# A two-layer hybrid decoder kernel: page copies spread over attention, early-turned key steps taken together, value weights split early, a fourth value slot

## The chip, the cores and the metric

The kernel runs on one NeuronCore of a Trainium2 chip. Time is device microseconds (us) of one execution; three executions of the kernel before took 1945.38 to 1946.76 us, median 1946.29. A further execution was taken by the hardware profiler; it took 1943.64 us, and its trace covers a span of 1942.0 us.

The engines are called by the profile's names: PE (TensorE, matrix products) and PEld (its weight loads), DVE (VectorE), ACT (ScalarE), POOL (GpSimd) and SP (SyncE). SP and POOL issue nearly all DMA transfers, each on a queue of its own: the profile calls SP's q1 and POOL's q0.

## The reference

Two layers of a decoder work on 512 prompt rows and on 32 sample rows (8 sequences of 4 tokens). Each has a combined input projection, a retention branch, a block-sparse attention branch (MoBA) with rotary positions, two gates, an output projection and a SwiGLU feed-forward part. Only the attention of the sample rows reads the paged cache:

```python
def moba_sample(q, k_new, v_new, k_pages, v_pages, page_table):
    ...
    def one(q_b, kn_b, vn_b, pt_b):
        ...
            k_full = k_pages[pt_b[:n_full * ppb]].reshape(n_full, M_BLOCK, M_HEADS, M_DH)
            means = jnp.mean(k_full.astype(jnp.float32), axis=1).swapaxes(0, 1)
            idx, valid = moba_select(qh, means, n_full_q, k_sel)
            phys = pt_b[idx[..., None] * ppb + jnp.arange(ppb)]
            kg = k_pages[phys, :, hidx].reshape(M_HEADS, L, k_sel, M_BLOCK, M_DH)
            vg = v_pages[phys, :, hidx].reshape(M_HEADS, L, k_sel, M_BLOCK, M_DH)
        return moba_core(qh, kg, vg, valid, k_own, v_own, own_mask)
```

Each sequence has 8 pages of 128 tokens (8 heads of 64, fp32), so a page is 256 KB. All scores of all pages are computed; the choice of blocks (3 of 4 for each head and query) is made on the scores, and blocks that are not chosen get a large negative bias before the softmax. The new keys and values of prompt and sample are outputs of their own (`k_prompt`, `v_prompt`, `k_sample`, `v_sample`).

## The kernel before, in words

**Products.** fp32 products are made as three products of rounded parts: high weight with high input, low weight with high input, high weight with low input. A *unit* of weights (1024 rows by 256 columns) is loaded into one of two slots of `RAW` by SP (`full`, L536 on), its high part `WH` is written by ACT and its low part `WL` by DVE (the two calls named `split`, L1472 and L2023). A unit then serves five *tiles* of outputs, four of 128 prompt rows (24 matmuls each) and one of the 32 sample rows (16 short ones, `sample_part`, L817). The units of the first half of a layer are, in this order: `mqk` (4 units), `mv` (2), `rqa` (1), `rv` (4), `rqb` (3), then `br_att` and others.

**Page copies.** A step `r` of keys (16 in a layer, r = 0 to 15) takes one page of each of 4 sequences. POOL copies each page of keys from the cache to a DRAM tensor `keys_laid` in another layout (`lay_keys`, L673 to L679), 64 copies in a layer, and counts their landings in two semaphores, one for the 12 copies of steps 0 to 2 (`FIRST_STEPS`, 3) and one for the other 52. In layer 0 they stand at the start (L683 to L686): the first 12 wait for nothing, the others for the tiles of `mqk` and `mv`, two copies to a tile. Layer 1's copies are made during layer 0's feed-forward part. After layer 0's 64 copies stand, in POOL's queue, the writes of the outputs `k_prompt`, `v_prompt`, `k_sample` and `v_sample` (L690 to L697).

**Key steps.** SP loads a laid step (1 MB) into one of four buffers (`keys(r)`, L567 to L576; buffers `PG` twice, `XT`, `PGK`), DVE turns it in place (`turned(r)`, L2095 to L2098), and PE multiplies it with the sample queries (`key_scores(q)`, L1069 to L1083). Steps 0 to 2 are loaded and turned before attention begins. `keys(3)` waits for all 52 later copies and for the last scores of the prompt's attention; `keys(r)` from 4 on waits for PE's `key_scores(r - 4)`.

**Order around the change.** All of it is written out by hand for each engine. After `mv`, PE transposes the rotated queries and keys (L952, L955), then runs the prompt's attention in 16 steps (`scores`, L1007; `turn_probs`, L1021; `attend`, L1037) with the tiles of `rqa` between them. ACT makes the exponentials (`exp`, L1529) and waits before the first one for the landing of `k_prompt` (L1536), since the probabilities overwrite its source. After the last attention step PE runs 16 key steps with tiles of `rv` between them (`value_rows`, which gives the tiles of a step), then 16 value steps (`attend_sample`, L1112) with tiles of `rqb` between them. The bank of an `rqa` tile is freed by ACT (`to_rotate`, L1494) into one of two buffers, which DVE then rotates (`rotated`, four instructions, L2050 to L2055). `attended(3)` (L1540 on ACT, L2136 on DVE) splits the last attention output into parts.

**Value steps.** `values` (L509 to L523) loads the value pages of a step into one of three slots, two sequences by SP and two by POOL; from step 3 on each load waits for PE's value step three before it. `own_head` (L2197) and `to_columns` (L1126) finish a group of 4 sequences.

## Time and profile before

| | |
|---|---|
| Three executions | 1945.38, 1946.29, 1946.76 us |
| Profiled execution, its own time | 1943.64 us |
| Span of its trace | 1942.0 us |
| PE busy | 1904.5 us, 98% |
| DVE, ACT, POOL busy | 1331.9, 815.6, 203.9 us |
| DMA, whole span | 300.60 MB, mean 155 GB/s |
| Chain that ended last | PE 66%, DVE 5%, issue, DMA and ACT 1% each |

Busy time of PE is time in which some matmul is under way; the rest of the span, some 37 us, is time in which PE had nothing. A matmul record is longer than the distance between two matmuls, since they overlap, so distances between starts are used for what work costs. In a row of a timeline the first number is the start, the second the length of the merged piece, and what stands in brackets is how long the engine was idle before it and what ended that idle time.

### The profile page before, as it was taken

How to read it: one execution, taken by the hardware profiler on the slowest of the kernel's cores; microseconds unless marked ns; L12 is line 12 of the kernel's file. 1: busy time of each engine (PE TensorE's matmuls, PEld its weight loads, DVE VectorE, ACT ScalarE, POOL GpSimd, SP SyncE). 2: the span in 40 equal slices, each digit the busy share in tenths (PEclk: the TensorE clock that was granted, in tenths of full speed). 3: DMA queues.
4: the chain of work that ended last, by engine and by line, in shares of the span. 5: the costliest groups of instructions: out<-in, count | busy, mean ns of one | idle time of the engine just before them, and what ended most of it. 6: DMA issues, size and time to landing. Idle time of an engine off the chain costs nothing.

```text
span 1942.0 us, 39546 instructions
## 1 busy us (share of the span) xinstructions
PE 1904.5 (98%) x16267; PEld 1784.2 (92%) x16267; DVE 1331.9 (69%) x1902; ACT 815.6 (42%) x1287; POOL 203.9 (10%) x293
## 2 busy tenths in 40 slices
PE   8889999999999999999999999999999999999999
PEld 8867978999999999999999688799899999999998
DVE  6466744347765988988665775543686668889876
ACT  4344333323434454554433632233244345455453
POOL 2520020012000002112100002100110000000000
PEclk9999999999999999999999999999999999999999
DMA  7944883246244346656453278622642442433332
GB/s 244 353 156 159 298 288 104 68 150 220 77 155 133 87 126 182 182 161 185 137 190 134 63 249 285 219 72 83 210 139 93 150 133 77 144 94 103 100 102 85
DMA packets 274852, 300.60 MB, mean 155 GB/s; under 512 B 14538, under 2 KB 225650, under 8 KB 274162
## 3 DMA queue, kind: packets, MB, share of 16 engines
q1 hardware_dynamic: 249202, 207.48, 34.0%
q0 software_dynamic: 25344, 90.46, 14.1%
q8 instruction: 129, 2.11, 0.5%
q14 instruction: 49, 0.40, 0.1%
q10 hardware_dynamic: 128, 0.15, 0.0%
HBM read 273.00 MB, written 58.59 MB: 171 GB/s over the span
## 4 chain that ended last, share of the span: by engine, by line
PE 66%; DVE 5%; issue 1%; DMA 1%; ACT 1%; POOL 0%; SPq 0%; POOLq 0%; DVEq 0%; ACTq 0%
PE PS L913 26%; PE PS L1378 22%; PE PS L1289 3%; PE PS L893 2%; PE PS L894 1%; PE PS L895 1%; PE PS L872 1%; PE PS L873 1%; PE PS L874 1%; PE PS L1082 1%; PE PS L817 1%; PE PS L1112 1%; PE PS L1037 1%; PE PS L1432 0%; PE PS L1007 0%
## 5 line engine op out<-in xcount | busy, mean ns | idle before, releaser
L2023 DVE TENSOR_TENSOR WL<-RAW,WH 128x2048 fp32r<-128x2048 f32 (+2 forms) x76 | 161.0, 2119 | 68.0 <-ACT WH L1472 68.0
L913 PE MATMUL PS<-XH,WH 128*128 128x272 f32 x960 | 203.2, 293 | 0.6
L913 PE MATMUL PS<-XL,WH 128*128 128x272 f32 x960 | 198.4, 288 | 0.0
L913 PE MATMUL PS<-XH,WL 128*128 128x272 f32 x960 | 197.8, 287 | 0.0
L1472 ACT ACTIVATE WH<-RAW 128x2048 fp32r<-128x2048 f32 (+2 forms) x84 | 149.8, 1783 | 34.7 <-PE PS L913 18.5
L1378 PE MATMUL PS<-KQ,CH 128*128 128x272 f32 x1088 | 158.3, 288 | 1.4 <-DVE KQ L2609 1.4
L913 PEld LDWEIGHTS PS<-XH,WH 128*128 128x128 f32 x960 | 150.4, 188 | 7.8 <-issue 5.2
L893 PE MATMUL PS<-WH,XH 128*128 128x256 f32 x512 | 152.3, 297 | 4.5 <-ACT EA L1494 4.5
L913 PEld LDWEIGHTS PS<-XL,WH 128*128 128x128 f32 x960 | 150.9, 188 | 0.0
L913 PEld LDWEIGHTS PS<-XH,WL 128*128 128x128 f32 x960 | 150.3, 189 | 0.0
L1378 PEld LDWEIGHTS PS<-KQ,CH 128*128 128x128 f32 x1088 | 145.0, 188 | 2.2 <-issue 2.2
L894 PE MATMUL PS<-WL,XH 128*128 128x256 f32 x512 | 145.9, 285 | 0.0
L895 PE MATMUL PS<-WH,XL 128*128 128x256 f32 x512 | 145.0, 283 | 0.0
L893 PEld LDWEIGHTS PS<-WH,XH 128*128 128x128 f32 x512 | 97.5, 190 | 31.7 <-issue 27.6
L678 POOL DMA_DIRECT2D keys_laid<-in_cache_k x128 | 95.3, 744 | 212.7 <-issue 198.1
L872 PE MATMUL PS<-WH,XH 128*128 128x256 f32 x336 | 96.7, 288 | 5.4 <-ACT EA L1505 5.4
L895 PEld LDWEIGHTS PS<-WH,XL 128*128 128x128 f32 x512 | 98.2, 192 | 0.0
L894 PEld LDWEIGHTS PS<-WL,XH 128*128 128x128 f32 x512 | 97.6, 191 | 0.0
L873 PE MATMUL PS<-WL,XH 128*128 128x256 f32 x336 | 96.1, 286 | 0.0
L874 PE MATMUL PS<-WH,XL 128*128 128x256 f32 x336 | 95.3, 284 | 0.0
L1859 ACT ACTIVATE EB<-PS 128x272 f32<-128x272 f32 x96 | 38.1, 397 | 129.7 <-PE PS L1378 127.6
L2621 DVE TENSOR_TENSOR CH<-RAW,CH 128x1536 fp32r<-128x1536 f32 x44 | 77.2, 1755 | 12.5 <-ACT CH L1841 12.5
(462 smaller groups left out, 5116.0 us busy)
## 6 DMA issues: line engine op xcount, KB each, us to landing
RAW<-in_w_in SPq DMA_DIRECT2D x94, 512.0 KB, 5.8
keys_laid<-in_cache_k POOLq DMA_DIRECT2D x128, 256.0 KB, 4.5
RAW<-in_w_gu SPq DMA_DIRECT2D x128, 256.0 KB, 4.3
PG<-keys_laid SPq DMA_DIRECT2D x16, 1024.0 KB, 6.5
RAW<-in_w_down SPq DMA_DIRECT2D x64, 256.0 KB, 4.3
RAW<-in_w_gu SPq DMA_DIRECT2D x24, 512.0 KB, 5.1
PG<-in_cache_v POOLq DMA_DIRECT2D x44, 256.0 KB, 4.8
PG<-in_cache_v SPq DMA_DIRECT2D x44, 256.0 KB, 4.5
```

The lines of the kernel that those rows point to most:

```text
L678: pool.dma_start(KEYS.ap()[lay, r, b].rearrange("(g k) (c d) -> (k c) g d", g=4, c=4), src.rearrange("p (g d) -> p g d", g=4)).then_inc(ke ...
L872: pe.matmul(out, a, wh[:, k], start=k == 0, stop=False)
L873: pe.matmul(out, a, wl[:, k], start=False, stop=False)
L874: last = pe.matmul(out, b, wh[:, k], start=False, stop=k == KT - 1)
L893: pe.matmul(out, a, wh[:, k], start=k == 0, stop=False)
L894: pe.matmul(out, a, wl[:, k], start=False, stop=False)
L895: last = pe.matmul(out, b, wh[:, k], start=False, stop=k == KT - 1)
L913: last = pe.matmul(PS[:, 2 * pair + h, 0:HALF], w[:, i, c0:c0 + P], block[:, h * HALF:(h + 1) * HALF], start=first and i == 0 and a == 0, ...
L1378: last = pe.matmul(PS[:, bank, 0:HALF], a[:, k, :], moving(n - 1, k, low), start=start and k == m == 0, stop=k == HK - 1 and m == 2, skip_ ...
L1472: act.activation(WH[:, slot, 0:n], RAW[:, slot, 0:n], ACT.Copy).then_inc(hi_ready, 1)
L2023: dve.tensor_tensor(WL[:, slot, 0:n], RAW[:, slot, 0:n], WH[:, slot, 0:n].bitcast(F32), ALU.subtract).then_inc(lo_ready, 1)
L2621: dve.tensor_tensor(a_part(s, 1), raw_chunks(s % 2)[:, 1:4], a_part(s, 0).bitcast(F32), ALU.subtract).then_inc(la_ready, 1)
```

## The change

Five things change, in both layers unless it is said otherwise.

1. Layer 0's page copies. The first 34 of the 64 are issued during `mqk` and `mv`; the first 12 of them now wait for tiles too, two to a tile, and from the 13th on it is one to a tile rather than two. The other 30 (`late`) stand behind the writes of the four outputs and wait for the prompt's attention scores, two to a step.
2. PE runs the key steps 0, 1 and 2 one after the other, then the last `rqa` tile, then `rv` tiles, 19 of them spread evenly over key steps 3 to 15.
3. The first `rv` unit is split before attention: ACT before its first exponential, DVE between taking the norm factors and the first reciprocals. The later splits move from key steps 1, 5, 9, 13 to 4, 7, 10, 14.
4. DVE waits for the last attention product, rotates three tiles and then does `attended(3)`; ACT does `to_rotate(2)` before its `attended(3)`. In the value steps `own_head(0)` stands ahead of the rotation of step 8.
5. Value step 3 goes to a fourth slot (`PGK`), with all four sequences loaded by SP; the steps from 4 on use the three slots in turn, and steps 4 to 6 wait for value steps 0 to 2.

```diff
-        return V_STEP // 4 * 16 + (32 * len(range(slot, V_STEP, 3)) if slot < 3 else 0)
+    def value_place(v):
+        return v if v < 4 else (v - 4) % 3
...
     def value_rows(q):
-        return [q - 1 + u for u in range((q + 3) // 4 - (q % 4 == 1), (q + 3) // 4 + 1)] if q else []
+        n = V_STEP - FIRST_STEPS
+        return range((q - FIRST_STEPS) * (4 * TT - 1) // n, (q + 1 - FIRST_STEPS) * (4 * TT - 1) // n) if q >= FIRST_STEPS else ()
...
-            if v < 3:
+            if v < 4:
                 hold(eng, sc_done, scores_done(lay, V_STEP - 4 + v))
-            for b in seqs:
-                if v >= 3:
-                    hold(eng, pvs_page, lay * 64 + 4 * (v - 3) + b + 1)
+            for b in seqs if v != 3 else range(GRP) if eng is nc.sync else ():
+                if v >= 4:
+                    hold(eng, pvs_page, lay * 64 + 4 * (v - (4 if v < 7 else 3)) + b + 1)
...
-                for at_r, name, j, col in ((4, "rv", 1, C_RV), (7, "rv", 2, C_RV), (10, "rv", 3, C_RV),
+                for at_r, name, j, col in ((4, "rv", 1, C_RV), (7, "rv", 2, C_RV), (11, "rv", 3, C_RV),
...
-        for i in range(GRP * V_STEP):
-            if i >= GRP * FIRST_STEPS:
-                hold(pool, tile_done, T0["mqk"] + 2 + (i - GRP * FIRST_STEPS) // 2)
+        early, late = GRP * FIRST_STEPS, 2 * 15
+        for i in range(GRP * V_STEP - late):
+            hold(pool, tile_done, T0["mqk"] + (i // 2 if i < early else i - early // 2))
             lay_keys(0, i)
...
+            for i in range(late if lay == 0 else 0):
+                hold(pool, s_done, i // 2 + 1)
+                lay_keys(0, GRP * V_STEP - late + i)
             values(pool, lay, (2, 3), page_in_b)
...
-                if q == 1:
+                if q == FIRST_STEPS:
                     token_part("rqa", 4, kk)
...
+            split(U0["rv"], 1, 8 * UC, (tile_done, lay * NT + T0["rqa"]))
             act.wait_ge(kp_out, lay * 16 + 16)
...
-            attended(3)
...
             to_rotate(2)
+            attended(3)
             to_rotate(3)
-            split_at(U0["rv"])
...
-                if q in (1, 5, 9, 13):
-                    split_at(U0["rv"] + (q + 3) // 4)
+                if q in (4, 7, 10, 14):
+                    split_at(U0["rv"] + (q - 1) // 3)
...
             take_rt(2 * lay + 1, (6, 7))
+            split(U0["rv"], 1, 8 * UC)
...
-            attended(3)
...
+            dve.wait_ge(pv_done, lay * 4 + 4)
             rotated(0)
             rotated(1)
             rotated(2)
-            split_at(U0["rv"])
+            attended(3)
             rotated(3)
             turned(3)
...
             for i in range(V_STEP):
+                if i == 8:
+                    own_head(0)
                 for f in late_rows(i):
                     rotated(f)
```

On DVE, at the end of the prompt's attention, the program before has these rows (`MOL` is the low part that `attended` writes, the `EA` and `RQ` rows are one `rotated`, `WL` is a split, `PGK` the turn of key step 3; two more rotations stand before the split and one behind it):

```order
L2136 TENSOR_TENSOR MOL<-PS,MOH 128x512 x2
L2050 SCALAR_TENSOR_TENSOR EA<-EA,CL 128x128
L2051 TENSOR_TENSOR EA<-EA,CL 128x128
L2052 TENSOR_TENSOR EA<-EA,CL 128x256
L2055 TENSOR_TENSOR RQ<-EA 128x256
...
L2023 TENSOR_TENSOR WL<-RAW,WH 128x2048
...
L2097 STREAM_TRANSPOSE PGK<-PGK 128x2048
```

The changed program has at the same place (`MOL` at L2149, a rotation at L2063 to L2068; between the first rotation and the second `MOL` row stand two more):

```order
L2149 TENSOR_TENSOR MOL<-PS,MOH 128x512
L2063 SCALAR_TENSOR_TENSOR EA<-EA,CL 128x128
L2064 TENSOR_TENSOR EA<-EA,CL 128x128
L2065 TENSOR_TENSOR EA<-EA,CL 128x256
L2068 TENSOR_TENSOR RQ<-EA 128x256
...
L2149 TENSOR_TENSOR MOL<-PS,MOH 128x512
L2063 SCALAR_TENSOR_TENSOR EA<-EA,CL 128x128
...
L2110 STREAM_TRANSPOSE PGK<-PGK 128x2048
```

The split is gone from this place, the second `MOL` stands behind three rotations, and the turn of key step 3 has four rotations and a `MOL` ahead of it.

On PE, at the end of the prompt's attention, the program before goes on as follows (`PT,MV` is the last attention product, `QB` rows are key steps, the `WH` row begins the last `rqa` tile and `RAW,XT` is the sample tile of `rv`):

```order
L1037 MATMUL PS<-PT,MV 64x128 [waits pt_evac]
L1037 MATMUL PS<-PT,MV 64x128 x7
L1082 MATMUL PS<-PG,QB 32x128 [waits s_exp,kt_turned]
L1082 MATMUL PS<-PG,QB 32x128 x15
L893 MATMUL PS<-WH,XH 128x256 [waits tile_free,lo_ready]
...
L817 MATMUL PS<-RAW,XT 32x256 [waits xn_ready,tile_free,lo_ready]
```

The changed program:

```order
L1049 MATMUL PS<-PT,MV 64x128 x7
L1094 MATMUL PS<-PG,QB 32x128 [waits s_exp,kt_turned]
L1094 MATMUL PS<-PG,QB 32x128 x15
L1094 MATMUL PS<-PG,QB 32x128 [waits kt_turned]
...
L1094 MATMUL PS<-XT,QB 32x128 [waits kt_turned]
...
L905 MATMUL PS<-WH,XH 128x256 [waits tile_free,lo_ready]
...
L829 MATMUL PS<-RAW,XT 32x256 [waits xn_ready,tile_free,lo_ready]
L829 MATMUL PS<-RAW,XT 32x256 x7
L1094 MATMUL PS<-PGK,QB 32x128 [waits kt_turned]
```

Key steps 1 and 2 stand directly behind step 0, and key step 3 (`PGK`) behind one `rqa` tile and the sample tile of `rv`.

On POOL the changed program of layer 0 has, where before a last copy stood ahead of `out<-QK` and value loads behind `out<-MVS`:

```order
L687 DMA keys_laid<-in_cache_k 128x4x128
L699 DMA out<-QK 128x4x512 [waits rot_free]
L702 DMA out<-MV 128x4x512 [waits tile_free]
L705 DMA out<-XT 32x512 [waits own_act]
L706 DMA out<-MVS 32x512
L518 TENSOR_LOAD PTAB [waits s_done]
```

The last row begins the first of the 30 late copies.

## Rows read from the trace of the kernel before

**Rows 1.** The page: busy us of each engine, share of the span, instructions.

```profile
PE 1904.5 (98%) x16267; PEld 1784.2 (92%) x16267; DVE 1331.9 (69%) x1902; ACT 815.6 (42%) x1287; POOL 203.9 (10%) x293
```

**Rows 2.** Waits of PE: in total, times, longest, us.

```profile
PE PS L1007 <- ACT PR L1529: 6.8, 6, 5.1
PE PS L872 <- ACT EA L1505: 5.4, 1, 5.4
PE PS L893 <- ACT EA L1494: 4.5, 2, 2.3
...
PE PS L1112 <- DMA PG<-in_cache_v: 2.1, 2, 1.1
...
PE PS L817 <- DVE WL L2023: 1.9, 2, 1.0
...
PE PS L1126 <- DVE OS L2197: 1.4, 2, 0.7
...
PE PS L1112 <- DMA XT<-in_cache_v: 0.3, 1, 0.3
```

**Rows 3.** Timeline of PE: start, length, idle before.

```profile
110.78 1.04 PE L980 MATMUL PS<-XT,STK 128*32 128x512 f32 x2
...
164.93 1.08 PE L1082 MATMUL PS<-PG,QB 128*32 128x128 f32 x32
...
168.28 0.36 PE L893 MATMUL PS<-WH,XH 128*128 128x256 f32 x1 [2.27 <-ACT EA L1494]
...
173.71 1.07 PE L817 MATMUL PS<-RAW,XT 128*32 128x256 f32 x16 [1.04 <-DVE WL L2023]
...
1063.02 1.05 PE L980 MATMUL PS<-XT,STK 128*32 128x512 f32 x2
...
1111.25 1.08 PE L1082 MATMUL PS<-PG,QB 128*32 128x128 f32 x32
```

**Rows 4.** Timeline of ACT: the two long waits of layer 0.

```profile
59.03 1.91 ACT L1472 ACTIVATE WH<-RAW 128x2048 fp32r<-128x2048 f32 x1 [12.36 <-DMA RAW<-in_w_in]
...
121.50 0.37 ACT L1529 ACTIVATE PR<-PS,SM 128x128 f32<-128x128 f32 x1 [9.05 <-DMA out<-QK]
```

**Rows 5.** Timeline of POOL: the last copy, then the first output.

```profile
113.61 0.74 POOL L678 DMA_DIRECT2D keys_laid<-in_cache_k  x1 [0.40 <-issue]
114.35 0.81 POOL L690 DMA_DIRECT2D out<-QK  x1
```

**Rows 6.** Stretches: busy us of PE, PEld, DVE, ACT, POOL; PEclk, DMA share, GB/s.

```profile
61.50:67.00 5.50, 5.50 (x28) 5.26 (x32) 5.19 (x14) 1.13 (x3) 3.50 (x5) 0.50 1.03 394
...
169.70:173.00 3.30, 2.97 (x15) 2.67 (x13) 2.26 (x3) 1.92 (x2) 0.00 (x0) 0.50 0.26 102
...
300.00:306.00 6.00, 4.76 (x43) 2.35 (x35) 2.79 (x7) 0.82 (x3) 0.00 (x0) 1.00 0.61 207
```

**Rows 7.** Timeline of DVE at the end of layer 0's attention.

```profile
165.68 0.69 DVE L2136 TENSOR_TENSOR MOL<-PS,MOH 128x512 fp32r<-128x512 f32 x1 [7.25 <-ACT MOH L1540]
...
167.67 0.29 DVE L2050 SCALAR_TENSOR_TENSOR EA<-EA,CL 128x128 f32<-128x128 f32 x1
...
174.77 2.30 DVE L2097 STREAM_TRANSPOSE PGK<-PGK 128x2048 f32<-128x2048 f32 x1
```

**Rows 8.** The page copies issued from 29 to 57 us: shortest, median, longest ns.

```profile
L678 POOL DMA_DIRECT2D keys_laid<-in_cache_k x22: 742/742/923, 30.2 to 56.8; - x22
```

**Rows 9.** The page's DMA issues: KB each, median us from issue to landing.

```profile
keys_laid<-in_cache_k POOLq DMA_DIRECT2D x128, 256.0 KB, 4.5
...
PGK<-keys_laid SPq DMA_DIRECT2D x8, 1024.0 KB, 7.5
```

**Rows 10.** DMA queues from 30 to 60 us: packets, MB, share.

```profile
q1 hardware_dynamic: 4103, 5.52, 53.2%
q0 software_dynamic: 1610, 5.29, 46.2%
```

**Rows 11.** DVE's groups from 113 to 165 us.

```profile
L2149 DVE TENSOR_SCALAR PR<-PR,SM 128x128 f32<-128x128 f32 (+3 forms) x32 | 10.9, 384 | 0.6
```

More of the change, by code:

```diff
@@ L449, in key_buf, with values_before, slot_values @@
         return PAGE_BUFS[q % 4]
-    def slot_total(slot):
-        return V_STEP // 4 * 16 + (32 * len(range(slot, V_STEP, 3)) if slot < 3 else 0)
+    def value_place(v):
+        return v if v < 4 else (v - 4) % 3
+    def values_before(v):
+        return [value_place(w) for w in range(v)].count(value_place(v))
+    def slot_values(slot):
+        return [value_place(v) for v in range(V_STEP)].count(slot)
     def key_landings(lay, q):
-        return lay * slot_total(q % 4) + (q // 4 + 1) * 16
+        return lay * (V_STEP // 4 * 16 + (32 * slot_values(q % 4) if q % 4 < 3 else 64)) + (q // 4 + 1) * 16
     def value_slot(lay, v):
-        slot, landed_b = v % 3, 32 * len(range(v % 3, V_STEP, 3))
-        return (slot, PAGE_BUFS[slot], lay * slot_total(slot) + V_STEP // 4 * 16 + (v // 3 + 1) * 32,
-                lay * landed_b + (v // 3 + 1) * 32)
+        slot = value_place(v)
+        landed_b = 32 * (lay * slot_values(slot) + values_before(v) + 1)
+        return slot, PAGE_BUFS[slot], (lay + 1) * V_STEP // 4 * 16 + landed_b * (2 if v == 3 else 1), landed_b
     def scores_done(lay, q):
@@ L1109, in attend_sample @@
                 pe.wait_ge(page_in[slot], landings)
-                pe.wait_ge(page_in_b[slot], landings_b)
+                if slot < 3:
+                    pe.wait_ge(page_in_b[slot], landings_b)
                 for b in range(GRP):
@@ L2233, in _ @@
             for q in range(V_STEP):
-                if q in (1, 5, 9, 13):
-                    split_at(U0["rv"] + (q + 3) // 4)
+                if q in (4, 7, 10, 14):
+                    split_at(U0["rv"] + (q - 1) // 3)
                 if q == N_PAGES:
@@ L2253, in _ @@
                     sample_probs_turned(1)
-                if i == 8:
-                    own_head(0)
                 if i == 10:
```

## The prediction, written before the changed kernel ran

> **What bounds the kernel now.** The page comes first: PE is busy for 98% of the span [rows 1], and the change leaves the work of every matmul as it is. So it can give back only two things: time in which PE stands idle, about 37 us in all (the span less PE's busy time), and time in which its clock is at the lower of its two levels. The list of PE's waits says where the idle time is; the reader is to see seven rows that lie in the stages the change touches [rows 2]. The timelines of PE and ACT then give each one its place and its cause.
>
> - A. Layer 0, before its 15th tile: PE waits 5.44 us for ACT, and ACT has waited 12.36 us for a unit of weights [rows 2, 4]. POOL issued 22 page copies in the 26.6 us before it [rows 8], and from 30 to 60 us both queues moved about the same, 5.52 and 5.29 MB, at 99% of the engines' time [rows 10].
> - B. Layer 0, first exponentials: ACT stands 9.05 us until `k_prompt` has landed [rows 4]. POOL could issue that write only at 114.35, behind its 64th copy [rows 5]. PE loses 5.1 us to it [rows 2].
> - C. After attention, both layers: 2.27 us for ACT's freeing of an `rqa` bank, then some 1 us for the split of the first `rv` unit [rows 2, 3]. ACT had to wait for DVE's first rotation, which stands behind `attended(3)`, and DVE for ACT's high part of that output [rows 7].
> - D. `to_columns(0)` waits 0.7 us in each layer for `own_head`; value pages cost 2.1 and 0.3 us [rows 2].
>
> The stretches tell what a long stall costs on top: after A (61.5 to 67) and after C (169.7 to 173) the granted clock is 0.50, that is 1.2 of 2.4 GHz; after the 1.1 us stall for a value page at 300 to 306 it stays at 1.00 [rows 6].
>
> **The copies (B).** In the changed order 34 copies stand ahead of `k_prompt` instead of 64, and the 34th waits for the 27th of 30 tiles, three tiles of 2.9 us before the transposes. The write is issued before 100 us, where the old one needed 121.5 - 114.4 = 7.1 us to land [rows 4, 5], and is there before ACT asks for it at about 113. What is late next? Layer 1 shows it, since its copies are made elsewhere and it has no such wait: from the last sample product ahead of attention to the first key step takes 1111.25 - 1063.02 = 48.2 us there and 164.93 - 110.78 = 54.2 us in layer 0 [rows 3]. I take layer 1's length for layer 0: **5.9 us** gained, with the clock's share in it. Bounds: 5.1 (the wait alone) and 6.9 (what ACT loses, were all of it PE's).
>
> What the thirty late copies cost: they have nobody behind them on POOL but value loads that come 75 us later. Their customer is `keys(3)` on SP. POOL starts them at about 113.6; in the stretch shown POOL needs (56.8 - 30.2) / 21 = 1.27 us a copy, 38 us for thirty, about as long as attention's 16 steps last, so POOL sets the pace and the thirtieth is issued by 113.6 + 30 x 1.27 = 151.7 and landed 4.5 us later, at 156.2 [rows 8, 9]. The first key step would now be at 159.0 (110.8 + 48.2). `keys(3)` lands 7.5 us after its issue, at 163.7 [rows 9]; DVE wants it at 159.0 + 5.9 = 164.9 (next part). It is in time with 1.2 us to spare, so I cost this at nothing; every us beyond is a us of PE. The first twelve copies' new waits are met before POOL comes to them.
>
> **The copies (A).** Do fewer copies bring the late weights sooner? The 13th to 20th copy wait for the 6th to 13th tile, done by the time POOL, at 1.27 us a copy, gets there; the 21st waits for the 14th, after which PE stops, 5.4 us before ACT's split and the release behind it, at about 56 [rows 2, 4]. Before, the 22nd went out at 56.8 [rows 8]. So until 56 the load is the same, what is then queued lasts for several us more (5.29 MB in 30 us is a copy in 1.5 us), and the weights landed at 59.0 [rows 4]. I take **0** here; bounds 0 and 8.2 us: 5.4, and 2.8 for the 5.5 us at half clock behind it [rows 6]. The trace has the two queues in nearly equal parts while both have work [rows 10]. The Trainium skill says why (DMA: Bandwidth & Descriptors, Queues, rings and completion order): each DMA engine goes round the queue rows that have work, a packet at a time. By that rule too a shorter copy queue helps only from the moment it runs empty, which is after these weights have landed; the trace agrees as far as it goes.
>
> **Key steps 0 to 2 together, the early split, DVE's order (C).** From the first key step to the first `rv` tile took 173.71 - 164.93 = 8.78 us [rows 3]. The work in it is one key step of 1.0 and one `rqa` tile. That tile ran 168.28 to 172.67, of which 1.4 us at full clock and 3.0 at half: 2.9 us of full clock. So 8.78 - 3.9 = 4.9 us are lost, clock included; layer 1 has both waits too [rows 2].
> Now, counted from the first key step: PE has three key steps (3.0), the tile (2.9) and the sample tile of `rv` (1.0), and comes to key step 3 at 6.9. ACT needs one rotation of DVE to free the bank, at about 2.0, before the tile's turn at 3.0; the `rv` unit is split since attention. What is late next is the turn of key step 3. DVE starts its first rotation when the last attention product ends, at 0.1. A rotation takes 1.38 from start to start (166.29 to 167.67, where 166.29 is the `MOL` start plus the 0.61 before its successor) and 1.2 when something independent follows; so three take 4.0, `attended(3)` 0.6, the fourth 1.2, and the turn starts at 5.9 and ends at 8.2 [rows 7]. PE waits 8.2 - 6.9 = 1.3 us where it lost 4.9: **3.6 us a layer, 7.2 in all**. Bounds for the new wait: 0, and 2.3, the longest wait of the old place [rows 2].
> Does a stall of 1.3 us lower the clock? 2.27 did, 1.1 did not [rows 2, 6]; 1.3 is nearer to the second. I take no; each lowering would cost 1.7 us (3.3 us at half clock) [rows 6].
> The split moved ahead of attention costs ACT 1.9 us before its first exponential and DVE 2.3 us before its first reciprocals. It lies beside the `rqa` tile of 2.9 us that PE runs there, and DVE's next task, the maximum of step 2, waits for PE's scores after that tile. I take 0, bounds 0 and 1 us a layer. The later splits have two key steps of lead, 8 us against 4.2.
>
> **Value steps (D).** `own_head(0)` no longer stands behind a rotation of 1.2 us: **1.4 us** for both layers. The wait of 0.3 us is for value step 5 of layer 1, which is now asked for one step earlier: **0.3 us**. The 2.1 us are for the last step, whose load still waits for value step 12: nothing. Bounds for these together 0 and 3.8.
>
> **Sum.** 5.9 + 7.2 + 1.4 + 0.3 = 14.8 us. Against the profiled execution's 1943.64 that is 1928.8; the median of the runs is 2.65 us higher, 1946.29, so I forecast **1931.5 us**.
>
> **Rivals.**
> 1. *The new stalls before key step 3 lower the clock.* For it: 2.27 us did. Against: 1.1 us did not. Both layers: 3.4 us back, 1934.9.
> 2. *The weights of A come sooner.* For it: POOL's queue has half the traffic, so anything that thins it before 41 us would do. Against: the 21st copy is the first that is held. 8.2 us more, 1923.3.
> 3. *Layer 0's attention does not become layer 1's.* `k_prompt` is still late, or exponentials and copies disturb each other; B gives nothing: 1937.4.
> 4. *The late copies hold up key step 3: slower.* Their end governs `keys(3)`. With 1.2 us to spare, each us later costs PE one. The gain is eaten when they end 14.8 + 1.2 = 16 us late, at 1.27 + 16/30 = 1.8 us a copy; 3.9 us more, 1950.2, at 1.93. For it: no trace shows copies beside attention. Against: 742 ns is both the shortest and the median record of a copy, under full DMA load [rows 8].
> 5. *DVE's scalings hold POOL up, in part.* DVE scales the probabilities 32 times in attention, 10.9 us [rows 11]. If POOL can't work beside them, the copies end 10.9 us later and PE waits 10.9 - 1.2 = 9.7 us more: 1941.2. For it: POOL's waits of this kind would show nowhere before. Against: POOL's 22 copies ran beside a busy DVE without a slow one [rows 8]. The Trainium skill has such a rule (SBUF — State Buffer, SBUF: two separate sides): while DVE runs an operation in a two-port mode, GpSimd can't write the descriptors of its transfers. No row here shows a copy beside such a scaling.
>
> **How the numbers follow.** Forecast 0.66, its own range 1929 to 1934 (B's and D's bounds, and the wait from 0 to 2.3). Rival 1: 0.10. Rival 2: 0.06. Rival 3: 0.06. Rival 4: 0.05. Rival 5: 0.07. Ends of the range: 1926.5, which keeps a part of rival 2, and 1938.5, which takes in rivals 1 and 3. About 0.2% (3.9 us) is what a measurement can tell from no change. Faster: all but rival 4 and a worse form of rival 5, 0.93; same 0.03; slower 0.04.
>
> **What would show it.** Right: `k_prompt` lands before 108 us and ACT has no DMA wait before the first exponential; the distance of B's two landmarks is near 48 us in both layers; the last late copy lands before 157; the key step from `PGK` has an idle time of about 1.3 us on PE, ended by DVE's turn, and no half clock behind it; the wait before the 15th tile is still 5.4 us; `to_columns(0)` waits no more. Wrong: a DMA wait ahead of that turn on DVE in layer 0 (rival 4), PE's clock at 0.50 at about 168 or 1110 us (rival 1), a shorter wait of ACT for its fourth unit (rival 2), or new waits among the `rv` tiles, where I have seen none.

## The result, and the profile after

The changed kernel takes **1925.3 us** (median of 4 runs: 1926.76, 1924.51, 1924.94, 1925.65), the kernel before beside it 1945.84 (1943.08 to 1946.76); ratio 0.9898 (of the means, as all ratios here), 95% interval 0.9881 to 0.9915. The forecast was 1931.5 and its range ended at 1926.5: the direction held and so did the mechanisms that were named, but the gain was larger by 6.2 us.

The profiled execution took 1926.76 us, its span is 1925.1. The page, as in [rows 1]:

```profile
PE 1897.3 (99%) x16267; PEld 1781.5 (93%) x16267; DVE 1332.1 (69%) x1902; ACT 814.2 (42%) x1287; POOL 201.4 (10%) x289
```

PE's idle time fell from 37.5 to 27.8 us, and PE's busy time fell too, by 7.2 us, with the same 16267 matmuls: that second part is clock and something else, which the experiments name. PE's waits, against [rows 2]:

```profile
PE PS L884 <- ACT EA L1518: 5.4, 1, 5.4
...
PE PS L1094 <- DVE PGK L2110: 2.8, 2, 1.4
PE PS L1019 <- ACT PR L1542: 2.4, 6, 0.5
PE PS L1125 <- DMA XT<-in_cache_v: 2.2, 2, 1.4
```

The wait A before the 15th tile stands as it was. The 5.1 us before the first exponentials, the waits of 2.27 and 1.0 us after attention and the two for `own_head` are gone. What is new is the wait of 1.4 us before key step 3 (line 1094, once a layer), and the last value step's page, now in `XT`. The timeline of PE gives the landmarks of [rows 3]:

```profile
109.33 1.05 PE L992 MATMUL PS<-XT,STK 128*32 128x512 f32 x2
...
157.66 1.96 PE L1094 MATMUL PS<-PG,QB 128*32 128x128 f32 x64
...
165.93 1.08 PE L1094 MATMUL PS<-PGK,QB 128*32 128x128 f32 x32 [1.41 <-DVE PGK L2110]
...
1050.25 1.04 PE L992 MATMUL PS<-XT,STK 128*32 128x512 f32 x2
...
1098.46 1.95 PE L1094 MATMUL PS<-PG,QB 128*32 128x128 f32 x64
...
1230.39 1.07 PE L1125 MATMUL PS<-XT,PTS 128*32 128x512 f32 x8 [1.44 <-DMA XT<-in_cache_v]
```

With the same landmarks of before, the two profiled executions compare so (us; "key and value part" runs from the first key step to the first transpose of the retention queries, at 303.69 and 1250.23 before, 290.96 and 1232.37 after):

| stretch | before | after | gained |
|---|---|---|---|
| start to the last sample product, layer 0 | 110.78 | 109.33 | 1.45 |
| attention, layer 0 | 54.15 | 48.33 | 5.82 |
| key and value part, layer 0 | 138.76 | 133.30 | 5.46 |
| from there to layer 1's attention | 759.33 | 759.29 | 0.04 |
| attention, layer 1 | 48.23 | 48.21 | 0.02 |
| key and value part, layer 1 | 138.98 | 133.91 | 5.07 |
| rest | 691.77 | 692.73 | -0.96 |
| span | 1942.00 | 1925.10 | 16.90 |

The loss of 0.96 at the end has a place. Behind the 1.44 us wait for the last value page the granted clock of PE was at the lower of its levels for a while, and not at all behind the 1.41 us wait before key step 3. Columns: busy us of PE, PEld, DVE, ACT, POOL; granted clock (0.5 is 1.2 of 2.4 GHz), DMA share, GB/s, as in [rows 6].

```profile
1232.40:1235.80 3.40, 3.40 (x22) 3.40 (x18) 1.54 (x3) 0.69 (x2) 0.00 (x0) 0.51 0.00 1
165.00:169.00 4.00, 3.07 (x49) 2.87 (x50) 3.97 (x6) 0.07 (x1) 0.00 (x0) 1.00 0.99 364
```

POOL's timeline and then DVE's answer to [rows 5, 7]. `k_prompt` is issued at 96.81 (it landed at 103.1), before ACT's first exponential at 112.71, which waits for no DMA. The thirty late copies go out from 112.95 to 148.07, one in 1.21 us. DVE's rotations start when attention ends, and its turn of the page for key step 3 at 163.57:

```profile
96.81 0.81 POOL L699 DMA_DIRECT2D out<-QK  x1
...
112.95 0.77 POOL L687 DMA_DIRECT2D keys_laid<-in_cache_k  x1 [0.62 <-issue]
...
148.07 0.78 POOL L687 DMA_DIRECT2D keys_laid<-in_cache_k  x1 [0.59 <-issue]
```

DVE, the first rotation and the turn:

```profile
157.78 0.29 DVE L2063 SCALAR_TENSOR_TENSOR EA<-EA,CL 128x128 f32<-128x128 f32 x1 [6.55 <-PE PS L1049]
...
163.57 2.30 DVE L2110 STREAM_TRANSPOSE PGK<-PGK 128x2048 f32<-128x2048 f32 x1
```

### The profile page after: what moved, and what is told of

It is laid out like the page before. It is cut to its first block and busy times, and to the rows that moved or that the text cites. A ratio compares the mean times of both kernels' runs of the same rounds, so it can differ in the third digit from the quotient of the medians.

```text
span 1925.1 us, 39547 instructions
## 1 busy us (share of the span) xinstructions
PE 1897.3 (99%) x16267; PEld 1781.5 (93%) x16267; DVE 1332.1 (69%) x1902; ACT 814.2 (42%) x1287; POOL 201.4 (10%) x289
```

## Experiments

Waits and clocks below are those of each kernel's profiled execution; times are medians. Over all five sets the kernel before gave medians of 1945.84, 1942.75, 1943.05, 1943.08 and 1941.68 (single runs from 1938.11 to 1947.49), so single executions scatter by some 9 us, and medians of 4 to 15 of them by 4. In the text, *half clock* is a stretch with a granted clock of 0.5.

**The changed kernel again** (no edit).

> The changed kernel once more, for a second profile and more times beside the kernel before. Theory M (the parts add up: copies 5.8 us, key steps 4.5 us a layer, own_head 1.4, value slots about 0): the mean gain is 17 to 20 us. The profiled changed run lost 1.1 us to a half-clock piece behind a 1.44 us value wait of layer 1. Theory L (that piece is a matter of the single execution): the same wait of 0.7 to 1.5 us is there again, the half clock behind it may be missing, and the run is then about 1.5 us shorter. Rival: the wait of 1.44 always lowers the clock, the piece is there again and the time is 1926.5 again.

1924.51 us against 1942.75, ratio 0.9901 (0.9886 to 0.9916): 18.2 us, inside theory M's 17 to 20. In its profile the last value step of layer 1 waited 1.91 us, and the lower clock behind it lasted twice as long:

```profile
1230.80 1.07 PE L1125 MATMUL PS<-XT,PTS 128*32 128x512 f32 x8 [1.91 <-DMA XT<-in_cache_v]
```

The stretch behind it, with the columns of [rows 6]:

```profile
1232.60:1239.40 6.80, 6.80 (x45) 5.53 (x42) 2.36 (x6) 1.37 (x4) 0.00 (x0) 0.50 0.00 1
```

Of the retention transposes behind it, the stretch up to 1240.86 took 7.90 us, where the same took 5.39 in a profile without a fall of the clock. The first profile of the same kernel has 6.54 there. So theory L is half right: from one execution to the other the wait grew by 0.5 us and the cost of the clock from 1.15 to 2.5. But the half clock came again, as the rival had it; that such a wait can stand without it shows only further down, with the write of x moved.

**The copies alone** (the kernel before, with the edits to `lay_keys`' two loops only).

> The kernel before with only the copies of layer 0 spread out. Theory M: 5.8 us faster than before (ratio 0.9970), all of it between the last sample product ahead of attention (110.8 us in before) and the first key step: that distance falls from 54.2 to 48.3 us; ACT's wait for the landing of k_prompt is gone. Rival (the copies' spreading also frees the start or the weights before tile 15): more than 7 us. Rival (it only helps together with the rest, as the first key steps wait for something): under 3 us. The waits of 2.27 and 1.0 us after attention stay.

1935.27 us, ratio 0.9956 (0.9943 to 0.9970), 5.8 to 11 us. The interval alone would leave room for the rival above 7 us, the landmarks don't: attention of layer 0 took 48.33 us (110.07 to 158.40) where it took 54.15, 5.8 us, as in the changed kernel, and the start ahead of it gained 0.7. The waits after attention stayed, the second of them longer than before:

```profile
161.75 0.36 PE L896 MATMUL PS<-WH,XH 128*128 128x256 f32 x1 [2.27 <-ACT EA L1497]
...
167.18 1.32 PE L820 MATMUL PS<-RAW,XT 128*32 128x256 f32 x16 [2.34 <-DVE WL L2026]
```

The copies are independent of the rest, and their price is the one read from layer 1. The longer second wait is not their doing: it is 2.33 us in the profile of the value steps alone, too, where the copies are as before. And behind the first of the two, of 2.27 us, the clock did not fall here, as it did in [rows 6]; it fell only behind the second:

```profile
161.75:167.40 5.65, 3.31 (x28) 3.05 (x32) 4.47 (x9) 2.75 (x3) 0.00 (x0) 1.00 0.44 168
```

**The key steps alone**, on the kernel before: PE's order, and DVE's (ACT's has the same two moves), with the new `value_rows` and the split times that go with it.

```diff
-                if q == 1:
+                if q == FIRST_STEPS:
                     token_part("rqa", 4, kk)
...
+            split(U0["rv"], 1, 8 * UC)
             for s in range(16):
...
-            attended(3)
...
             rotated(2)
-            split_at(U0["rv"])
+            attended(3)
```

> The kernel before with only the three key steps together, the early split of the first value unit, DVE's and ACT's attended(3) behind three rotations, and the new spread of the rv tiles over the key steps. Theory M: 9.0 us faster (ratio 0.9954): 3.5 a layer from the waits (4.9 lost before, 1.4 new) and 1.0 a layer from three fewer changes between dense tiles and the narrow matmuls of the key steps, at 0.3 us each. Rival (my predicted sum): 7.2 us, the rest of the gain came from somewhere else, as from the value part. The new 1.4 us wait before key step 3 is there in both layers, without half clock.

1932.66 us, ratio 0.9950 (0.9937 to 0.9964), 9.7 us. The new wait of 1.40 us is there in both layers without a fall of the clock. The key and value part of layer 0 took 133.43 us instead of 138.76: 5.3 us, of which 0.9 from the last value page (its wait was 0.19 us, before 1.08) and **4.4 from the edit**, not the 3.6 that I had worked out. Where PE isn't waiting, these stretches show it as busy; in the kernel before:

```profile
164.93:303.69 138.76, 133.69 (x1557) 108.71 (x1555) 83.51 (x136) 39.40 (x70) 17.57 (x32) 0.99 0.81 270
```

in the changed one:

```profile
157.66:290.96 133.30, 131.15 (x1557) 107.75 (x1555) 81.32 (x135) 37.47 (x69) 16.18 (x30) 1.00 0.84 285
```

and in this one it is 131.14. The same 1557 records of matmuls take 133.7 or 131.1 us. About 1.6 of the 2.5 is the half clock of [rows 6] (3.3 us at half speed). The other 0.9 went with the order: in the timelines I count 29 blocks of dense tiles between the narrow matmuls of the key and value steps before, and 25 after. One such change of work, in the changed kernel's timeline (start, length):

```profile
283.11 1.06 PE L1125 MATMUL PS<-PG,PTS 128*32 128x512 f32 x8
284.11 0.38 PE L905 MATMUL PS<-WH,XH 128*128 128x256 f32 x1
284.33 0.28 PE L906 MATMUL PS<-WL,XH 128*128 128x256 f32 x1
284.45 0.28 PE L907 MATMUL PS<-WH,XL 128*128 128x256 f32 x1
...
286.95 0.27 PE L907 MATMUL PS<-WH,XL 128*128 128x256 f32 x1
287.16 1.06 PE L1125 MATMUL PS<-PG,PTS 128*32 128x512 f32 x8
```

Dense matmuls start every 0.12 us. The first of a block takes 0.22, and the first narrow one behind a block starts 0.21 after the last dense one: 0.1 and 0.1 us lost, 0.2 a block, shown nowhere as a wait. It is so at all 25 blocks of this stretch. A new tile inside a block costs nothing of the kind, 0.11 us from the last matmul of one to the first of the next, so the loss belongs to the change of work and not to the start of a tile:

```profile
194.13 0.27 PE L907 MATMUL PS<-WH,XL 128*128 128x256 f32 x1
194.24 0.28 PE L905 MATMUL PS<-WH,XH 128*128 128x256 f32 x1
```

What in PE takes the 0.2 us no run shows.

**The value steps alone** (fourth slot and `own_head(0)` ahead, on the kernel before).

> The kernel before with only the fourth value slot and own_head(0) ahead of the late rotation. Theory M: 1.4 us from to_columns, which waits no more; the value slots give between 0 and 0.5: 1.4 to 1.9 us faster (ratio 0.9991), under what can be told from no change. Rival (the fourth slot gives earlier landings that shorten the waits of 1.0 us at the last value steps): 3 us. The last value step still waits 0.7 to 1.5 us for its page in both.

1941.35 us against 1942.75, ratio 0.9995 (0.9984 to 1.0006): no difference that can be told. `to_columns` waits no more, 1.4 us; but in this profile the last value pages came later:

```profile
302.96 1.06 PE L1121 MATMUL PS<-XT,PTS 128*32 128x512 f32 x8 [2.00 <-DMA XT<-in_cache_v]
```

That wait and the half clock behind it (304.0 to 310.8 us) ate the gain.

**The write of x behind the fourth unit of weights.** Wait A was still whole. ACT's row for it, in the changed kernel:

```profile
58.17 1.91 ACT L1485 ACTIVATE WH<-RAW 128x2048 fp32r<-128x2048 f32 x1 [12.32 <-DMA RAW<-in_w_in]
```

On SP's queue a write stands ahead of the weights that ACT waits for; in the list of DMA issues from 29 to 60 us (KB, us to landing):

```profile
x_kept<-XT SPq DMA_DIRECT2D x1, 2048.0 KB, 21.2
```

The edit puts it behind them:

```diff
                 full(U0["mqk"] + 2 + j, j, w_in, KT, C_MQ + (2 + j) * UC)
-                if j == 0:
+                if j == 1:
                     sp.dma_start(XTD.ap()[:, :, 0:SEQ], XT[:, :, 0:SEQ]).then_inc(xt_kept, 16)
```

> The changed kernel with the write of x to its DRAM copy (2.1 MB) behind the fourth unit of weights instead of ahead of it on SP's queue. Theory Q (the weights before the 15th tile are late because of what stands ahead of them in their own queue, which moves about 0.18 MB a us beside POOL's copies): they land about 10 us sooner, PE's wait of 5.4 us is gone and the half clock behind it (6.8 us at half speed, some 2 to 3 us lost) too: 6 to 8 us faster than the changed kernel, ratio to before about 0.986. Rival (the write only moves the lateness to the next units, the mv weights at 82 us): a new wait of 3 to 5 us on PE before the 20th tile or later.

1918.63 us, ratio 0.9874 (0.9849 to 0.9899): 6 to 7 us under the changed kernel's two medians, 5 by the ratios. The split now waits for nothing, and key step 3 comes at 157.90 instead of 165.93, 8.03 us sooner, of which 5.40 are the wait and some 2.3 the 4.5 us of work at half clock behind it:

```profile
45.31 1.90 ACT L1485 ACTIVATE WH<-RAW 128x2048 fp32r<-128x2048 f32 x1
```

The half clock from 58.2 to 65.0 is gone with the wait, and nothing came late instead. Its last value step in layer 1 waited 1.43 us, as long as in the changed kernel, this time at full clock:

```profile
1222.26 1.06 PE L1125 MATMUL PS<-XT,PTS 128*32 128x512 f32 x8 [1.43 <-DMA XT<-in_cache_v]
```

The stretch behind it has a granted clock of 1.00:

```profile
1224.20:1227.60 3.40, 3.24 (x40) 3.02 (x40) 1.77 (x4) 1.37 (x4) 0.00 (x0) 1.00 0.01 4
```

**The early copies thinned.**

```diff
-            hold(pool, tile_done, T0["mqk"] + (i // 2 if i < early else i - early // 2))
+            hold(pool, tile_done, T0["mqk"] + (i if i < early else 15 + (i - early) // 2))
```

> The changed kernel with the early copies thinner: the first twelve one for each tile, the next 22 only from the 15th tile on, two a tile, so that ten fewer copies (2.6 MB) are issued before PE's wait at 55 us. Theory Q2 (the copies and the weights share the engines, half each): the weights land some 5 us or more sooner, PE's wait falls from 5.4 us to under 1 and its half clock goes: 5 to 8 us faster than the changed kernel. Rival (what is ahead in the weights' own queue decides, the copies don't matter): still 4 us or more of wait. Rival (the copies now end too late for k_prompt): ACT waits at 113 us again.

1920.89 us, ratio 0.9879 (0.9853 to 0.9906). The wait A fell from 5.4 to 0.5 us, its half clock went, and `k_prompt` was in time. So either end works: what stands ahead in the weights' own queue, or what runs beside it in the other. A wait of 1.09 us for the last value page did lower the clock here:

```profile
1224.03 1.07 PE L1125 MATMUL PS<-XT,PTS 128*32 128x512 f32 x8 [1.09 <-DMA XT<-in_cache_v]
```

The stretch behind that one, at 0.51:

```profile
1226.20:1229.60 3.40, 3.40 (x19) 3.40 (x19) 1.54 (x3) 0.69 (x2) 0.00 (x0) 0.51 0.00 0
```

**One rv tile more ahead of key step 3.**

```diff
-        return range((q - FIRST_STEPS) * (4 * TT - 1) // n, (q + 1 - FIRST_STEPS) * (4 * TT - 1) // n) if q >= FIRST_STEPS else ()
+        cuts = [0] + [max(2, j * (4 * TT - 1) // n) for j in range(1, n + 1)]
+        return range(cuts[q - FIRST_STEPS], cuts[q + 1 - FIRST_STEPS]) if q >= FIRST_STEPS else ()
```

> The changed kernel with one dense rv tile more ahead of key step 3, taken from the step behind it. Theory: the wait of 1.4 us before key step 3 is DVE's chain of rotations, and PE has 2.9 us of other work for it: the wait is gone in both layers, 2.8 us faster than the changed kernel; one change between dense and narrow matmuls fewer gives 0.3 a layer more: 3.4 in all. Rival (the key step waits for its page by then or the next steps are late instead): under 1.5 us.

1923.72 us, ratio 0.9899 (0.9874 to 0.9924): in time within the scatter of the changed kernel. The wait of 1.40 us went and a wait of 0.75 for DVE's turn of a later page came, in both layers: 0.65 us a layer, not 1.7. DVE's chain of turns is what is late, and moving one tile moves the place. The number of blocks stayed at 25, against what I had expected.

```profile
169.51 1.08 PE L1095 MATMUL PS<-PG,QB 128*32 128x128 f32 x32 [0.75 <-DVE PG L2111]
```

**Three value slots again, all else as changed.**

> The changed kernel with three value slots again, all else as changed (own_head(0) ahead of the late rotation too). Profiles so far: with three slots the last value step waited 0.2 to 1.1 us (1.08, 0.97, 0.66, 0.19, 0.82) without a half-clock piece behind it; with four 0.65 to 2.0 us (0.75, 1.44, 0.65, 1.91, 2.00, 1.07) and three times a half-clock piece. Theory F (the fourth slot lengthens the last wait): waits under 1.1 us in both layers, no half clock there, 1 to 3 us faster than the changed kernel (1922 to 1924). Theory L (the waits scatter, whatever the slots): waits and time as of the changed kernel, within 1 us.

1925.81 us, ratio 0.9905 (0.9888 to 0.9921): as the changed kernel. Theory F's gain of 1 to 3 us did not come, and the fourth slot is worth nothing that can be told in time. The waits for the last page were small here (0 and 0.50 us, and 0.80 at value step 5 of layer 1), as F had it; the combination below that has three slots too waited 1.37 us and lost clock. Theory L's "whatever the slots" isn't borne out by the profiles either: the last page cost 0.5 to 2.05 us in both layers together in the five with three slots, 1.1 in the mean, and 1.4 to 3.1 us, 2.2 in the mean, in the seven with four slots and no hold. That part of F stays open.

```profile
1230.69 1.06 PE L1116 MATMUL PS<-PG,PTS 128*32 128x512 f32 x8 [0.50 <-DMA PG<-in_cache_v]
```

**SP's later weights held until value step 14 is done.**

```diff
             values(sp, lay, (0, 1), page_in, next_unit)
+            hold(sp, pvs_page, lay * 64 + 4 * (V_STEP - 2) + 4)
             full(U0["br_att"] + 1, 1, w_br_att, 4, 0)
```

> The changed kernel with SP's weights behind the value loads (br_att unit 1 and all after it) held until value step 14 is done, so that they don't move beside the last page. Theory W (these weights take engines from POOL's two loads of the last page, which land last, at 1228.3 and 1230.25 us): the last wait falls by 0.7 us or more in both layers. Rival (POOL's loads are late by their own issue and the distance from step 12): no change. Cost of the hold, if the weights come late for the gate tiles: a new wait 20 us later.

1922.82 us, ratio 0.9892 (0.9875 to 0.9908), a time within the scatter of the changed kernel. Both last waits are gone and no new one came. In layer 1 the step (line 1126, `XT`) follows its neighbour directly:

```profile
1226.62 1.06 PE L1126 MATMUL PS<-PG,PTS 128*32 128x512 f32 x8
1227.50 1.04 PE L1126 MATMUL PS<-XT,PTS 128*32 128x512 f32 x8
```

POOL's two loads of this page in layer 1 took 6.0 us to land in the changed kernel, where they are issued at 1222.73 and 1223.91, and 3.6 us here, issued at 1221.46 and 1222.64; the lists of DMA issues have, first for the changed kernel (1220 to 1232 us), then for this one (1218 to 1230 us):

```profile
XT<-in_cache_v POOLq DMA_DIRECT2D x2, 256.0 KB, 6.0
XT<-in_cache_v POOLq DMA_DIRECT2D x2, 256.0 KB, 3.6
```

So it was the company on the DMA engines that made the last page late. The last step in the fourth slot, the other way to have its page earlier, has no time: the load would overwrite retention keys that DVE has written to that memory by then.

**The rv tiles in clumps, before every second key step.**

```diff
+        cuts = [(j + j % 2) * (4 * TT - 1) // (n + 1) for j in range(n + 1)]
+        return range(cuts[q - FIRST_STEPS], cuts[q + 1 - FIRST_STEPS]) if q >= FIRST_STEPS else ()
```

> The changed kernel with the 19 rv tiles put ahead of every second key step (2 or 3 at a time) instead of one or two ahead of each: 7 blocks of dense tiles among the 13 key steps instead of 13. Theory S (each change from narrow matmuls to dense ones and back costs 0.3 us): 6 fewer give 1.9 us a layer, the wait of 1.4 before key step 3 goes as well (two tiles ahead of it), though 0.7 may come back at key step 5: 5 us faster in all than the changed kernel. Rival (two key steps in a row are more than the pages' landings or DVE's maxima keep up with): new waits at the key steps of 1 us and more each, no gain or slower.

1924.37 us, ratio 0.9910 (0.9889 to 0.9930): no gain. The test of the 0.2 us is the stretch below, to be set beside the 131.15 us of the changed kernel: the same 1557 matmuls, both at full clock, 25 blocks against 21 by the timeline: 0.8 us for 4 blocks, 0.2 each. I had put 0.3 on a change and counted six. What it gave was lost in a new wait, for ACT's freeing of a bank when three tiles follow each other (2.14 us, both layers):

```profile
154.75:288.23 133.48, 130.35 (x1557) 107.44 (x1555) 81.33 (x135) 37.46 (x69) 16.18 (x30) 1.00 0.84 284
```

Its timeline of PE:

```profile
58.10 0.38 PE L885 MATMUL PS<-WH,XH 128*128 128x256 f32 x1 [2.72 <-ACT EA L1519]
...
200.94 0.36 PE L906 MATMUL PS<-WH,XH 128*128 128x256 f32 x1 [2.14 <-ACT XT L1602]
```

The first of these two rows is wait A, untouched by this edit, and 2.7 us less than in the changed kernel. Over the ten profiles in which the early copies and weights are as before or as changed it was 2.7 to 6.4 us. The second, though as long as some waits of the kernel before that lowered the clock, did not lower it, in either layer:

```profile
200.94:207.00 6.06, 6.06 (x97) 5.46 (x97) 5.07 (x5) 1.30 (x3) 0.00 (x0) 1.00 0.81 263
```

**Write of x, tile, and three slots together.**

> The changed kernel with the write of x behind the fourth unit, one rv tile more ahead of key step 3, and three value slots again. By the parts: 8.0 (write) + 1.3 (tile) + 1 to 3 (slots) faster than the changed kernel's 1924.9: 1912.5 to 1914.5. Rival (the slots give nothing): 1915.5.

1916.80 us, ratio 0.9858 (0.9842 to 0.9875). The parts of the write and the tile add up to within 1.3 us (1915.5 was forecast from them alone); the last value page of layer 1 came 1.37 us late, with half clock behind it: the rival, that the slots give nothing, held.

```profile
1221.34 1.07 PE L1117 MATMUL PS<-PG,PTS 128*32 128x512 f32 x8 [1.37 <-DMA PG<-in_cache_v]
```

**Write of x, tile, and the held weights, with four slots.**

> The changed kernel with four value slots and three edits: the write of x behind the fourth unit of weights, one rv tile more ahead of key step 3, and SP's later weights held until value step 14 is done. By the parts as measured in the profiles: the write gives 8.0 us (5.4 of wait and the half clock behind it), the tile 0.65 a layer, the hold the last value waits (0.7 and 1.4) and their half clock (1.1 where it comes): 11.5 us faster than the changed kernel's 1924.9, so 1913.4. Rival (the last waits scatter and were small in e10 by chance): up to 1.9 us of wait there again, 1915 to 1917.

**1914.55 us** (1913.88 to 1914.69), ratio 0.9859 (0.9843 to 0.9876): 10.8 us under the changed kernel's 1925.3, 7.6 by the two ratios, and the lowest time here; by ratio it equals the combination before (0.9858), so that no time shows what the hold adds. It lies between the forecast of 1913.4 and the rival's 1915 to 1917, but the rival's waits for the last page did not come: they are gone in both layers, as in the kernel with the hold alone. Its four runs lie within 0.8 us, where those of the other kernels lie 2 to 9 apart. That the waits that it lacks, A and the last page, are what scatters fits this, but four runs don't show it. Its longest waits:

```profile
PE PS L799 <- DMA FIX<-in_consts_fixed: 3.1, 1, 3.1
PE PS L1021 <- ACT PR L1544: 2.4, 6, 0.5
PE PS L853 <- ACT WH L1474: 1.9, 1, 1.9
PE PS L1096 <- DVE PG L2112: 1.5, 2, 0.7
```

## Why the prediction was too small, step by step

- **The copies (B): right.** 5.8 us measured, 5.9 predicted, alone and with the rest. `k_prompt` landed at 103.1 (I had said before 108), the last late copy at 152.1 (before 157), `keys(3)` at 157.7, 5.8 us before DVE turned it, not 1.2: a copy took 1.21 us of POOL, not 1.27, and the page load behind them 5.6, not 7.5. Rivals 3, 4 and 5 fall with that: attention took 48.3 us beside thirty copies in layer 0 and 48.2 without any in layer 1. The Trainium skill's rule that POOL can't write descriptors while DVE is in a two-port mode (SBUF — State Buffer, SBUF: two separate sides) cost POOL nothing that can be seen: the copies kept their pace beside DVE's 32 scalings. What can be seen is a small cost on the other side. The scalings took longer beside the copies, by 33 to 54 ns each and 12.0 us in all instead of 10.9; first below is layer 0 of the changed kernel, then its layer 1, and the copies alone show the same. DVE's other operations in attention did not, and PE lost nothing by it. Whether this is the port of that rule at work no run shows.

```profile
L2163 DVE TENSOR_SCALAR PR<-PR,SM 128x128 f32<-128x128 f32 x8 | 2.1, 338 | 0.1
L2163 DVE TENSOR_SCALAR PR<-PR,SM 128x128 f32<-128x128 f32 x8 | 1.9, 284 | 0.1
```

- **The copies (A): right, at 0.** 5.40 and 5.34 us in the two profiles of the changed kernel, and the same half clock. Its upper bound of 8.2 us is about what the write of x gave when moved (8.0). Rival 2 named the way to it: fewer copies ahead of these weights, which the thinned early copies then showed (0.5 us of wait). The equal parts of [rows 10] are equal in MB, not in packets (4103 and 1610), so they don't by themselves bear out a turn by packets.
- **The key steps (C): this is a step that failed, a term too small by 1.8 us.** "PE waits 8.2 - 6.9 = 1.3 us where it lost 4.9: 3.6 us a layer". The new wait is 1.41 and 1.40 us, without half clock, as said. But the gain is 4.45 us in layer 0 (5.46 less 0.68 for `own_head` and 0.33 for the last page) and 4.56 in layer 1 (5.07 less 0.70, and 0.19 more for pages): 9.0 instead of 7.2. The term compared only the 8.78 us around the waits and took the rest of the rv tiles as unchanged ("new waits among the `rv` tiles, where I have seen none" was all I said of them). The changed `value_rows` lays 19 tiles over 13 steps, so that some stand next to each other, and the three key steps do too: four blocks fewer a layer at 0.2 us, a term that the prediction put at nothing without a reason. A list of waits can't show this, since the 0.2 us are busy time.
- **The value steps (D): 1.4 right, the rest scatter.** `to_columns` waits no more (0.68 and 0.70). The page waits were 1.08, 0.28 and 0.97 before and 0.75 and 1.44 after, 0.14 us in all; I had 0.3. What I had not priced is the clock behind such a wait: 1.15 us in the profiled run, 2.5 in the next.
- **The start: not predicted.** 1.45 us of the profiled difference lie before attention in layer 0, where the two kernels do nearly the same: 0.86 before tile 15 and the rest in how much work the half-clock stretch caught, about 4.5 us of it instead of the 5.5 and more of [rows 6]. The starts of the other profiles scatter as much, so I count it as chance, though no run isolates it.
- **The sum and the median: this step failed too, and by more, 4.1 us.** 14.8 predicted, 16.9 between the two profiled executions: 1.8 from C, 1.45 from the start, -0.96 from the last part, -0.2 from small ones. The remaining 4.1 of the 6.2 us lie in the last line, "the median of the runs is 2.65 us higher". Without them the forecast would have been 1927.4, 2.1 us from the measurement; with only C put right it would still have been 4.4 us off. I carried the distance of one execution from three others over as if it belonged to the kernel. It was scatter: later medians of the kernel before are 1941.7 to 1943.1, under its profiled 1943.64, and the changed kernel's median is 1.5 us under its profiled run. Against 1943.0 the gain is 18 us, of which the landmarks account for 16.3 (5.8 + 9.0 + 1.4 + 0.1); the ratio of the second set allows 16.3 to 22 us, so the remaining 2 are within the noise, and stay open.
- **Rival 1 (the new stalls lower the clock)** did not come before key step 3, in either layer of any of the seven profiles with a 1.4 us wait there. It did come at the last value step, a place that I had not put on the list. So my "no" was right for this place, but the reason given, that 1.3 us is nearer to 1.1 than to 2.27, was not: 1.09 us lowered the clock elsewhere, and 2.14 did not. That part was luck.

## What to carry to other kernels

On an engine that is busy all the time, count the changes between kinds of work as well as the waits: the busy time of the same instructions in a stretch, before and after, shows what a list of waits can't. When a wait is for a transfer, look at what stands ahead of it on its own queue and what runs beside it: one write put behind the weights that were waited for, and one hold on weights that nobody needed yet, gave most of what the last kernel gains in its profile over the changed one. And before a profiled execution is tied to a median, know how far single executions lie apart. Here the waits that came from a transfer scattered from profile to profile (2.7 to 6.4 us for A, 0.24 to 2.0 for the last page with four slots), while the one that came from DVE's chain was 1.40 or 1.41 us each time.

## What the runs showed of the hardware

- The length of a wait does not decide by itself whether the clock falls behind it. Waits of PE of 1.4 us before key step 3 never lowered it, at the last value step 1.43 and 1.39 did not, 1.44, 1.37 and 1.09 did, for 3.4 us, and 1.91 and 2.00 did for 6.8 us. Two of 2.14 us among the `rv` tiles did not, and the 2.27 us after attention did in four of six places. Where it fell behind a last value step the price was 1.1 to 2.5 us a time, about as much as the wait.
- A change between dense 128x256 tiles and narrow matmuls costs PE 0.2 us for a block of dense tiles between narrow ones, as busy time: 0.1 at the first dense matmul and 0.1 at the first narrow one (131.15 us for the same work with 25 blocks, 130.35 with 21).
- Thirty copies of 256 KB each, from DRAM to DRAM, did not slow attention beside them: 48.33 us in layer 0, against 48.21 in layer 1 without them. DVE's scalings alone took longer beside them, 12.0 us for 32 instead of 10.9.
- What moves beside a load makes it land later: POOL's last two page loads took 6.0 us with weights issued beside them, 3.6 without.
